# VectorE takes ten low-part subtractions of mixer 1 from GpSimd, woven between the conditioning sums

## The chip, the cores and the metric

The kernel runs on one core of one Trainium2 chip. The metric is the device time of one execution, in microseconds (us), median of several runs.

## What is computed

Two transformer blocks in a row, on 512 tokens of width 1024, all in float32. The part that this change touches is the end of the first block's mixer and the conditioning vector of the first block:

```python
mod = (c_act @ ada_w[l] + ada_b[l])[:, None, :]          # conditioning: 1024 -> 6144
sh_t, sc_t, g_t, sh_c, sc_c, g_c = jnp.split(mod, 6, axis=-1)
h = rms_norm(x, tm_pre_g[l]) * (1.0 + sc_t) + sh_t
...
gates = jax.nn.sigmoid(p["gate"] + merge_gate_b).reshape(Bn, S, N_BRANCH, D_MODEL)
merged = (gates[:, :, 0] * y_ml + gates[:, :, 1] * y_gla
          + gates[:, :, 2] * y_conf + gates[:, :, 3] * y_sc)
return merged @ w_o
```

## The kernel before, in words

**Units of weights.** Every large product runs over weight units of 128x2048 floats (1 MB). SP loads a unit into one of two buffers `w_raw` (512 KB per transfer, L481). ScalarE rounds it to the matmul format (`split`, L707, written `w_hi`), then VectorE or GpSimd computes the rest `w_lo = w_raw - w_hi`, its **low part** (`lo` in the kernel; L1731 on VectorE, L624 on GpSimd). TensorE multiplies high by high, high by low and low by high (L1209 to L1211: 48 matmuls of 512 columns per unit). Each buffer has two copies, so `w_hi` of unit u waits until TensorE has finished unit u-2 (`w_used`), and the load of unit u+2 waits for the low part of unit u (`parted`).

**The stage.** In program order the units here are `gate2` (4), `y2` (1), `gate0` (4), `y0` (1), `gate1` (4), `y1` (1), `wo` (4), then the feed-forward part `up1`. A `gate` unit yields two tiles of 128x512 in PSUM, which ScalarE opens with a sigmoid (`out_of`, L754). A `y` unit yields eight tiles; VectorE multiplies each with its gate (`gated`, L1982), which frees the PSUM bank, and adds it to `merged` (L1963). In `y1`, the last branch, ScalarE also rounds each merged tile (L953) and VectorE takes the merged tile's low part (L1968, `h_lo`), which `wo` needs. There are four PSUM banks for these tiles, so the fifth tile of a `y` unit waits for the product of the first.

**The conditioning sums.** The 6144 columns of `ada_w` are summed in 24 parts of 1 MB. Parts 0 to 7 are done at the start. Parts 8 to 23 are loaded by ScalarE's queue (L231, two transfers at a time, at places that the table `ADA_LOADED` gives), summed on VectorE (`ada_sum`: one L1769 and seven L1771 of 128x256 each, one after the other), and turned by TensorE (`ada_columns`, L1234, at places that `ADA_TURNED` gives). Four buffers hold parts, so loading part n from 12 on waits until TensorE has turned part n-4. TensorE waits in its own stream for a sum that isn't there.

**Who does what before.** GpSimd makes the low parts of all units from `y2` to the first `up1` unit. VectorE's queue has: `gated("y2")`, two `y_lo` subtractions, sums 8 to 13, `gated("y0")`, sums 14 to 21, `gated("y1")`, sums 22 and 23. All queues are in the order in which the code is written; nothing is reordered when it runs.

Of the kernel before, what the change touches and what calls it, by code (L numbers as in the profile page):

```python
# [149 lines left out]
def program(nc, A, out):  # L150
# [10 lines left out]
    with ctx:  # L161
        def sb(name, shape, dt=FP32):
            return ctx.enter_context(nc.sbuf_tensor(name, shape, dt))
# [3 lines left out]
        def sem(name):  # L167
            if name not in sems:
                sems[name] = ctx.enter_context(nc.semaphore(name))
            return sems[name]  # L170
# [9 lines left out]
        y_lo = sb("y_lo", [P, 4, S], F32R)  # L180
# [14 lines left out]
        def area(at, *shape):  # L195
            n = int(np.prod(shape))
            assert at + n <= WORK, (at, n)
            v = work[:, at:at + n]
            if len(shape) == 2:
                v = v.rearrange("p (a b) -> p a b", a=shape[0])  # L200
            if len(shape) == 3:
                v = v.rearrange("p (a b c) -> p a b c", a=shape[0], b=shape[1])
            return v
# [5 lines left out]
        def col(name, i=0, n=1):  # L209
            at = COLUMN[name]  # L210
            return par[:, at + i:at + i + n]
# [14 lines left out]
        def ada_place(n):  # L226

            return ada_first[n % 6] if n < 8 else ada_later[(n + 2) % 4]

        def ada_load(eng, n):  # L230
            eng.dma_start(ada_place(n), A["ada_w"][0][:, n * 2 * P:(n + 1) * 2 * P].rearrange("(k p) n -> p k n", p=P))\  # L231
               .then_inc(sem(f"ada_in{n % 8}"), 16)
# [7 lines left out]
        def vector_load(eng, g):  # L240
            r = 0
            for name, n in VECTORS[g]:
# [6 lines left out]
                else:  # L249
# [3 lines left out]

        ADA_LOADED = {(0, 0): (8, 9), (0, 1): (10, 11), (0, 2): (12, 13), (0, 4): (14, 15),
                      (1, 0): (16, 17), (1, 1): (18, 19), (1, 2): (20, 21), (1, 3): (22, 23)}
        ADA_TURNED = {(0, 2): (8, 9), (0, 3): (10, 11), (0, 4): (12, 13),
                      (1, 1): (14, 15), (1, 2): (16, 17), (1, 3): (18, 19), (1, 4): (20, 21)}
        ml_q, ml_k, ml_o = area(R, MT, S), area(R + 1024, MT, S), area(R + 2048, MT, S)  # L260
        ml_v = area(R + 3072, TT, MH * VW)
        ml_p, ml_h, ml_nm = area(R + 4128, 2, TT, S), area(R + 8224, TT, MIX), area(7232, S)
# [36 lines left out]
        def wait_full(eng, t, i=0):  # L299

            s, n, step = t.full
            eng.wait_ge(s, n + i * step)

        def wait_read(eng, t, i=0):

            eng.wait_ge(read[t.bank], t.n + i)
# [9 lines left out]
        def release(ins, t):  # L316
            ins.then_inc(read[t.bank], 1)
# [16 lines left out]
        U, unit = {}, 0  # L334
# [10 lines left out]
        def loaded_at(u):  # L345
            return 32 * (u // 2 + 1) + (16 if u >= IFA and (u - IFA) % 2 == 0 else 0)
# [260 lines left out]
        def _(pool):  # L607
# [13 lines left out]
            def lo(u):  # L621

                pool.wait_ge(hi_done, u + 1)
                pool.tensor_tensor(w_lo[u % 2][:, :], raw[u % 2][:, :], w_hi[u % 2][:, :].bitcast(FP32), ALU.subtract)\  # L624
                    .then_inc(parted[u % 2], 1)
# [20 lines left out]
                                       const("chunk_of").unsqueeze(2).broadcast_to([P, CPT, HD]), ALU.mult)\  # L646
                        .then_inc(sem("gl_placed"), 1)

            for u in range(U["y2"], U["up1"] + 1):
                lo(u)  # L650

            def hidden(n, conv_done):
# [45 lines left out]
        def _(act):  # L698
# [3 lines left out]
            def split(u, i=0, units=0):  # L702

                act.wait_ge(loaded[u % 2], loaded_at(u) + (i * 16 if units else 0))
                if u >= 2:
                    act.wait_ge(w_used, u - 1 + i)
                act.activation(w_hi[u % 2][:, :], raw[u % 2][:, :], ACT.Copy).then_inc(hi_done, 1)  # L707
# [41 lines left out]
            def out_of(t, dst, func, **kw):  # L749
                wait_full(act, t)  # L750
                src = bank[t.bank][:, :]
                if len(dst.shape) == 3:
                    src = src[:, 0:dst.shape[1] * dst.shape[2]].rearrange("p (a b) -> p a b", a=dst.shape[1])
                release(act.activation(dst, src, func, **kw), t)  # L754

            def gate_step(name, c, bias, u, used):

                split(u + 1)
                for k in range(2):
                    cc = 2 * c + k  # L760
                    if used is not None:
                        wait_read(act, T[used][cc])
                    out_of(T[name][cc], gates[:, cc, :], ACT.Sigmoid, **({} if bias is None else {"bias": col("merge_gate_b", bias + cc)}))
# [17 lines left out]
            u = U["sc"]  # L781
# [24 lines left out]
            u = U["ml"]  # L806
# [61 lines left out]
            u = U["gla"]  # L868
# [65 lines left out]
            def ada_more(b, c):  # L934

                for n in ADA_LOADED.get((b, c), ()):
                    if n == 8:
                        act.wait_ge(sem("y_lo"), 8)
                    if n >= 12:
                        act.wait_ge(sem("ada_turned"), n - 3)  # L940
                    ada_load(act, n)
# [260 lines left out]
        def _(pe):  # L1202
# [214 lines left out]
            def branch_unit(name, k0, n):  # L1417
                pe.wait_ge(sem("y_lo"), n)
                column_unit(U[name], T[name], 2, y_hi[:, k0:k0 + 2, :], y_lo[:, k0:k0 + 2, :])
# [90 lines left out]
            for k in range(2):  # L1510
                for c in range(4):
                    column_unit(U[f"gate{k}"] + c, T[f"gate{k}"][2 * c:2 * c + 2])
                    for p in ADA_TURNED.get((k, c), ()):
                        ada_columns(T["ada1"][0], p, 8)
                branch_unit(f"y{k}", 2 * k, 6 + 2 * k)
                for p in ADA_TURNED[(k, 4)]:
                    ada_columns(T["ada1"][0], p, 8)
# [207 lines left out]
        def _(dve):  # L1725
            ch = Chain(dve, "dve_step")

            def lo(u, i=0):

                dve.wait_ge(hi_done, u + 1 + i)  # L1730
                dve.tensor_tensor(w_lo[u % 2][:, :], raw[u % 2][:, :], w_hi[u % 2][:, :].bitcast(FP32), ALU.subtract)\  # L1731
                   .then_inc(parted[u % 2], 1)
# [33 lines left out]
            def ada_sum(n, unit):  # L1766

                dve.wait_ge(sem(f"ada_in{n % 8}"), 16 * (n // 8 + 1))
                ch.link(dve.tensor_scalar(unit[:, 0, :], unit[:, 0, :], c_act[:, 0:1], None, ALU.mult))  # L1769
                for k in range(1, KT):  # L1770
                    ins = dve.scalar_tensor_tensor(out=unit[:, 0, :], in0=unit[:, k, :], scalar=c_act[:, k:k + 1], in1=unit[:, 0, :],  # L1771
                                                   op0=ALU.mult, op1=ALU.add)
                    if k < KT - 1:
                        ch.link(ins)
                ins.then_inc(sem("ada_summed"), 1)
# [19 lines left out]
            u = U["sc"]  # L1795
# [160 lines left out]
            def product(c):  # L1956

                return rstd[:, :] if c % 3 == 2 else tbuf[:, c % 3, :]
# [8 lines left out]
                dve.wait_ge(sem("h_hi"), hn[0])  # L1967
                dve.tensor_tensor(h_lo[:, c, :], merged[:, c, :], h_hi[:, c, :].bitcast(FP32), ALU.subtract).then_inc(sem("h_ready"), 1)  # L1968

            def gated(name, bias=None, first=False, last=False):  # L1970

                for c in range(KT):
                    t = T[name][c]
                    wait_full(dve, t)
                    if GATE_OF[name] in ("gate2", "gp", "ga") or name == "y3" and c < KT - 1:
                        dve.wait_ge(sem(f"{GATE_OF[name]}_open"), c + 1)
                    else:
                        wait_read(dve, T[GATE_OF[name]][c])
                    dst = merged[:, c, :] if first else product(c)
                    if not first and gn[0] >= 2:  # L1980
                        dve.wait_ge(sem("added"), gn[0] - 1)
                    ins = dve.scalar_tensor_tensor(out=dst, in0=bank[t.bank][:, :], scalar=0.0 if bias is None else col(bias, c),  # L1982
                                                   in1=gates[:, c, :], op0=ALU.add, op1=ALU.mult)
                    release(ins, t)

                    if not first and c:
                        add(T[name][c - 1], c - 1)
                    if last and c >= 2:
                        merged_low(c - 2)
                if not first:  # L1990
                    add(T[name][KT - 1], KT - 1)
                if last:
                    for c in (KT - 2, KT - 1):
                        merged_low(c)
# [55 lines left out]
            for c in range(MT):  # L2050
# [17 lines left out]
                for hh in range(2):  # L2068
                    n = 2 * c + hh
# [6 lines left out]
                    release(dve.copy_predicated(gl_at[:, :, :], const("block_causal").bitcast(U32).unsqueeze(1).broadcast_to([P, TT, P]),  # L2076
                                                bank[t.bank][:, :].rearrange("p (a b) -> p a b", a=TT)), t)
            gla_norm(1)
            gated("y2", "conf_out_b")
            for k in range(2):  # L2080
                y_lo_of(gl_k[:, k, :], 2 + k, 7 + k)
            for n in range(8, 14):
                ada_sum(n, ada_place(n))
            gated("y0")
            for n in range(14, 22):
                ada_sum(n, ada_place(n))
            gated("y1", last=True)

            for n in (22, 23):
                ada_sum(n, ada_place(n))  # L2090
            ada_out(T["ada1"][0], 2 * KT, 4 * KT)
            wait_read(dve, T["ada1"][0])
            ch.tick(dve.tensor_tensor(gain[:, 1, :], mod[:, 2 * KT:3 * KT], col("tm_post_g", 0, KT), ALU.mult))
# [341 lines left out]
            for c in range(4):  # L2435
                for k in range(2):
                    t = T["wo2"][2 * c + k]
                    wait_full(dve, t)
                    n = 2 * c + k
# [59 lines left out]
```

## Time and profile before

| | us |
|---|---|
| median of 3 runs | 1729.02 |
| lowest, highest | 1725.0, 1729.88 |
| the profiled execution | 1726.85 |
| its span in the trace | 1724.9 |

The profiled execution is 2.2 us below the median. TensorE is busy for 95% of the span, VectorE for 55%, ScalarE for 35%, GpSimd for 18%. The mean granted TensorE clock is 0.967 of full speed. The stage of the change lies between about 398 and 560 us of the span. The views used are the list of waits, the timelines of the engines (start, length and, in square brackets, idle time before an instruction with what ended it), the chain of work that ended last, and the table by stretches.

### The profile page before, as it was taken

The page shows a single profiled execution, that of the slowest core. Times are in us where ns is not written, and L with a number is a line of the kernel's source. Part 1 is how long each engine was busy: PE and PEld are TensorE (multiplying, and loading weights), DVE is VectorE, ACT ScalarE, POOL GpSimd, SP SyncE. Part 2 cuts the span into 40 slices and gives each one's busy share as a digit, 9 for nine tenths or more (in the row PEclk, how much of TensorE's full clock was granted, in tenths as well). Part 3 has the DMA queues.
Part 4 walks back from the last instruction along what each step waited for, and adds up shares of the span by engine and source line. Part 5 has one row for each costly group of instructions (what it writes and reads, how often), then busy time and mean ns, then how long its engine had stood idle before and what let it go on. Part 6 is the DMA issues. An engine that isn't in the chain of part 4 may idle for free.

```text
span 1724.9 us, 19885 instructions
## 1 busy us (share of the span) xinstructions
PE 1636.9 (95%) x7592; PEld 1317.7 (76%) x7592; DVE 943.8 (55%) x1268; ACT 608.7 (35%) x758; POOL 310.0 (18%) x137
## 2 busy tenths in 40 slices
PE   5899999989899799999999899999999999999997
PEld 4688678768787578888888677877787888888886
DVE  4449456424989554444433657866434655556333
ACT  2342444224223443333322422344443433334222
POOL 0330013323343201111000000244353111111000
PEclk8799999988999999999999999999999999999999
DMA  8323122303764213333222224322122333332221
GB/s 284 108 79 99 49 74 74 94 30 108 234 225 134 79 51 97 97 97 97 98 98 97 74 77 124 90 74 74 50 74 75 108 98 97 97 97 97 98 97 49
DMA packets 192139, 170.41 MB, mean 99 GB/s; under 512 B 9413, under 2 KB 180973, under 8 KB 192077
## 3 DMA queue, kind: packets, MB, share of 16 engines
q1 hardware_dynamic: 174669, 150.39, 28.5%
q10 hardware_dynamic: 16800, 16.83, 3.1%
q0 software_dynamic: 608, 2.35, 0.4%
q8 instruction: 42, 0.69, 0.2%
q14 instruction: 20, 0.16, 0.0%
HBM read 165.54 MB, written 2.10 MB: 97 GB/s over the span
## 4 chain that ended last, share of the span: by engine, by line
PE 82%; DVE 10%; ACT 2%; issue 2%; SPq 2%; DMA 1%; POOL 0%; DVEq 0%; ACTq 0%
PE bank L1209 24%; PE bank L1211 23%; PE bank L1210 23%; DVE work L1771 4%; PE bank L1234 1%; SPq L231 1%; PE bank L1216 1%; DVE work L1834 1%; PE bank L1218 1%; PE bank L1217 1%; PE bank L1670 1%; ACT w_hi L707 1%; PE bank L1478 1%; PE bank L1308 1%; DVE w_lo L1731 1%
## 5 line engine op out<-in xcount | busy, mean ns | idle before, releaser
L1209 PE MATMUL bank<-h_hi,w_hi 128*128 128x512 f32 x1536 | 614.7, 400 | 26.3 <-DVE h_lo L1749 12.4
L1211 PE MATMUL bank<-h_hi,w_lo 128*128 128x512 f32 x1536 | 603.7, 393 | 0.0
L1210 PE MATMUL bank<-h_lo,w_hi 128*128 128x512 f32 x1536 | 603.7, 393 | 0.0
L1209 PEld LDWEIGHTS bank<-h_hi,w_hi 128*128 128x128 f32 x1536 | 291.9, 190 | 112.4 <-issue 38.6
L707 ACT ACTIVATE w_hi<-w_raw 128x2048 fp32r<-128x2048 f32 x131 | 250.1, 1909 | 304.8 <-PE bank L1211 257.3
L1211 PEld LDWEIGHTS bank<-h_hi,w_lo 128*128 128x128 f32 x1536 | 291.7, 190 | 62.7
L1210 PEld LDWEIGHTS bank<-h_lo,w_hi 128*128 128x128 f32 x1536 | 292.1, 190 | 59.3 <-issue 1.0
L1731 DVE TENSOR_TENSOR w_lo<-w_raw,w_hi 128x2048 fp32r<-128x2048 f32 x86 | 198.0, 2302 | 244.5 <-ACT w_hi L707 244.2
L624 POOL TENSOR_TENSOR w_lo<-w_raw,w_hi 128x2048 fp32r<-128x2048 f32 x45 | 210.0, 4666 | 513.1 <-ACT w_hi L707 512.9
L1209 PE MATMUL bank<-y_hi,w_hi 128*128 128x512 f32 x480 | 192.4, 401 | 13.1 <-DVE tbuf L1982 8.2
L1211 PE MATMUL bank<-y_hi,w_lo 128*128 128x512 f32 x480 | 189.7, 395 | 0.0
L1210 PE MATMUL bank<-y_lo,w_hi 128*128 128x512 f32 x480 | 189.7, 395 | 0.0
L660 POOL TENSOR_TENSOR work<-work 128x512 f32 x44 | 57.1, 1298 | 458.1 <-ACT work L1018 458.1
L1209 PEld LDWEIGHTS bank<-y_hi,w_hi 128*128 128x128 f32 x480 | 92.1, 192 | 36.1 <-DVE tbuf L1982 9.1
L1771 DVE SCALAR_TENSOR_TENSOR work<-work,small 128x256 f32<-128x256 f32 x154 | 112.8, 733 | 5.5
L1210 PEld LDWEIGHTS bank<-y_lo,w_hi 128*128 128x128 f32 x480 | 92.1, 192 | 19.5 <-issue 0.5
L1211 PEld LDWEIGHTS bank<-y_hi,w_lo 128*128 128x128 f32 x480 | 91.9, 191 | 19.6
L2166 DVE SCALAR_TENSOR_TENSOR work<-bank,par,work 128x511 f32<-128x511 f32 (+1 forms) x88 | 61.5, 743 | 77.8 <-ACT work L1012 77.8
L1012 ACT ACTIVATE work<-work,par 128x512 f32<-128x512 f32 x44 | 35.8, 815 | 106.8 <-DVE work L2155 106.8
L1012 ACT ACTIVATE work<-bank,par 128x512 f32<-128x512 f32 x44 | 30.0, 687 | 107.3 <-PE bank L1211 107.1
L2166 DVE SCALAR_TENSOR_TENSOR work<-work,par 128x511 f32<-128x511 f32 (+1 forms) x88 | 61.9, 746 | 9.6 <-ACT work L1012 9.6
L754 ACT ACTIVATE work<-bank,par 128x512 f32<-128x512 f32 x32 | 22.0, 687 | 119.1 <-PE bank L1211 119.1
(249 smaller groups left out, 1384.5 us busy)
## 6 DMA issues: line engine op xcount, KB each, us to landing
w_raw<-in_w_in SPq DMA_DIRECT2D x94, 512.0 KB, 4.7
w_raw<-in_ffn_w_up SPq DMA_DIRECT2D x44, 512.0 KB, 4.7
w_raw<-in_w_up SPq DMA_DIRECT2D x44, 512.0 KB, 4.9
work<-in_ada_w ACTq DMA_DIRECT2D x16, 1024.0 KB, 7.3
w_raw<-in_ffn_w_down SPq DMA_DIRECT2D x22, 512.0 KB, 3.9
w_raw<-in_w_down SPq DMA_DIRECT2D x22, 512.0 KB, 4.0
work<-in_ada_w SPq DMA_DIRECT2D x8, 1024.0 KB, 12.0
w_raw<-in_w_o SPq DMA_DIRECT2D x8, 512.0 KB, 4.0
```

The source lines that it names most:

```text
L231: eng.dma_start(ada_place(n), A["ada_w"][0][:, n * 2 * P:(n + 1) * 2 * P].rearrange("(k p) n -> p k n", p=P))\
L624: pool.tensor_tensor(w_lo[u % 2][:, :], raw[u % 2][:, :], w_hi[u % 2][:, :].bitcast(FP32), ALU.subtract)\
L660: pool.tensor_tensor(work[:, bass.ds(i * (2 * S) + k * S, S)], cbuf[:, k, 0, :], cbuf[:, k, 1, :], ALU.mult).then_inc(sem("hid" + n), 1)
L707: act.activation(w_hi[u % 2][:, :], raw[u % 2][:, :], ACT.Copy).then_inc(hi_done, 1)
L754: release(act.activation(dst, src, func, **kw), t)
L1012: act.activation(cbuf[:, k, part, :], src, ACT.Identity, scale=par[:, bass.ds(i * 2 + at, 1)], **kw).then_inc(sem("center" + n), 1)
L1209: pe.matmul(dst, w_hi[s][:, at:at + n], hi, start=first, stop=False)
L1210: pe.matmul(dst, w_hi[s][:, at:at + n], lo, start=False, stop=False)
L1211: return pe.matmul(dst, w_lo[s][:, at:at + n], hi, start=False, stop=last)
L1731: dve.tensor_tensor(w_lo[u % 2][:, :], raw[u % 2][:, :], w_hi[u % 2][:, :].bitcast(FP32), ALU.subtract)\
L1771: ins = dve.scalar_tensor_tensor(out=unit[:, 0, :], in0=unit[:, k, :], scalar=c_act[:, k:k + 1], in1=unit[:, 0, :], op0=ALU.mult, op1=ALU.add)
L2166: ins = dve.scalar_tensor_tensor(out=c[:, back:S], in0=src[:, 0:S - back], scalar=w, in1=c[:, back:S], op0=ALU.mult, op1=ALU.add)
```

## The change

VectorE now makes the low parts of eleven units in a row: `gate0` (4), `y0`, `gate1` (4), `y1` and the first of `wo`. GpSimd keeps `y2`, the other three of `wo` and the first of `up1`. On VectorE each low part stands between pairs of sums, and the low parts of `gate0`'s, `gate1`'s and `wo`'s first units stand inside `gated`, behind the fourth tile's product. The sums are the same 16, in other places: six between `y2` and `y0`, eight between `y0` and `y1`, two behind `y1`. The transfers of parts 8 and 9 are issued by ScalarE ahead of the first `gate0` tile, as soon as the two `y_lo` are there; those of 10 to 23 follow at earlier places than before or the same. TensorE turns parts 8 and 9 one unit earlier, and parts 14 to 21 as one, two, two, two, one in place of four pairs.

```diff
-        ADA_LOADED = {(0, 0): (8, 9), (0, 1): (10, 11), (0, 2): (12, 13), (0, 4): (14, 15),
-                      (1, 0): (16, 17), (1, 1): (18, 19), (1, 2): (20, 21), (1, 3): (22, 23)}
-        ADA_TURNED = {(0, 2): (8, 9), (0, 3): (10, 11), (0, 4): (12, 13),
-                      (1, 1): (14, 15), (1, 2): (16, 17), (1, 3): (18, 19), (1, 4): (20, 21)}
+        ADA_LOADED = {(0, 0): (10, 11), (0, 1): (12, 13), (0, 2): (14, 15), (0, 3): (16, 17),
+                      (1, 0): (18,), (1, 1): (19, 20), (1, 2): (21, 22), (1, 3): (23,)}
+        ADA_TURNED = {(0, 1): (8, 9), (0, 2): (10, 11), (0, 3): (12, 13), (0, 4): (),
+                      (1, 0): (14,), (1, 1): (15, 16), (1, 2): (17, 18), (1, 3): (19, 20), (1, 4): (21,)}
...
-            for u in range(U["y2"], U["up1"] + 1):
+            lo(U["y2"])
+            for u in range(U["wo"] + 1, U["up1"] + 1):
                 lo(u)
...
                 split(u + 1)
+                if u == U["gate0"]:
+                    act.wait_ge(sem("y_lo"), 8)
+                    for n in (8, 9):
+                        ada_load(act, n)
...
                     release(ins, t)
+                    if low_at and c == 3:
+                        lo(low_at)
...
-            gated("y2", "conf_out_b")
+            gated("y2", "conf_out_b", low_at=U["gate0"])
...
-            for n in range(8, 14):
-                ada_sum(n, ada_place(n))
-            gated("y0")
-            for n in range(14, 22):
-                ada_sum(n, ada_place(n))
-            gated("y1", last=True)
+            lo(U["gate0"] + 1)
+            sums(8, 9)
+            lo(U["gate0"] + 2)
+            sums(10, 11)
+            lo(U["gate0"] + 3)
+            sums(12, 13)
+            lo(U["y0"])
+            gated("y0", low_at=U["gate1"])
+            lo(U["gate1"] + 1)
+            sums(14, 15)
+            lo(U["gate1"] + 2)
+            sums(16, 17)
+            lo(U["gate1"] + 3)
+            sums(18, 19)
+            lo(U["y1"])
+            sums(20, 21)
+            gated("y1", last=True, low_at=U["wo"])
```

On VectorE, between the `y_lo` subtractions and the first product of `y0`, there stood six sums in a row (each a TENSOR_SCALAR and seven SCALAR_TENSOR_TENSOR); here the end of them, with the first product of `y0`:

```order
L1756 TENSOR_TENSOR y_lo<-work,y_hi 128x512 x2
L1769 TENSOR_SCALAR work<-work,small 128x256
L1771 SCALAR_TENSOR_TENSOR work<-work,small 128x256 x7
L1769 TENSOR_SCALAR work<-work,small 128x256
L1771 SCALAR_TENSOR_TENSOR work<-work,small 128x256 x7
...
L1982 SCALAR_TENSOR_TENSOR tbuf<-bank3,work 128x512
```

In the changed kernel the same place on VectorE reads (L1734 is the low part, L1772 and L1774 the sum, L1985 the product):

```order
L1759 TENSOR_TENSOR y_lo<-work,y_hi 128x512 x2
L1734 TENSOR_TENSOR w_lo1<-w_raw1,w_hi1 128x2048
L1772 TENSOR_SCALAR work<-work,small 128x256
L1774 SCALAR_TENSOR_TENSOR work<-work,small 128x256 x7
L1772 TENSOR_SCALAR work<-work,small 128x256
L1774 SCALAR_TENSOR_TENSOR work<-work,small 128x256 x7
L1734 TENSOR_TENSOR w_lo0<-w_raw0,w_hi0 128x2048
...
L1734 TENSOR_TENSOR w_lo0<-w_raw0,w_hi0 128x2048
L1985 SCALAR_TENSOR_TENSOR tbuf<-bank3,work 128x512
```

Four low parts (`gate0` units 1 to 3 and `y0`) now stand in that stretch, one ahead of each pair of sums and one behind the last.

On VectorE in the last branch, `gated("y1")`, a product, an addition (L1966) and a merged tile's low part (L1971) alternate; behind the fourth product stands now the low part of the first `wo` unit:

```order
L1985 SCALAR_TENSOR_TENSOR tbuf<-bank2,work 128x512
L1734 TENSOR_TENSOR w_lo0<-w_raw0,w_hi0 128x2048
L1966 TENSOR_TENSOR work<-work,rstd 128x512
L1971 TENSOR_TENSOR h_lo<-work,h_hi 128x512
L1985 SCALAR_TENSOR_TENSOR tbuf<-bank3,work 128x512
```

Before, the addition followed the product at once.

## Rows read from the trace of the kernel before

**Rows 1.** Waits of TensorE, 400 to 600 us: total, times, longest (us)
```profile
PE bank L1209 <- DVE tbuf L1982: 8.2, 2, 4.6
```
**Rows 2.** TensorE's timeline, unit `y0`: start, length, line, idle before
```profile
454.75 0.48 PE L1209 MATMUL bank<-y_hi,w_hi 128*128 128x512 f32 x1
...
465.03 0.50 PE L1209 MATMUL bank<-y_hi,w_hi 128*128 128x512 f32 x1 [4.55 <-DVE tbuf L1982]
...
465.96 0.63 PE L1209 MATMUL bank<-y_hi,w_hi 128*128 128x512 f32 x1
466.39 0.63 PE L1210 MATMUL bank<-y_lo,w_hi 128*128 128x512 f32 x1
...
472.20 0.95 PE L1234 MATMUL bank<-small,work 128*128 128x1 f32 x8
```
**Rows 3.** TensorE's timeline, unit `y1`
```profile
519.37 0.48 PE L1209 MATMUL bank<-y_hi,w_hi 128*128 128x512 f32 x1
...
528.76 0.79 PE L1209 MATMUL bank<-y_hi,w_hi 128*128 128x512 f32 x1 [3.66 <-DVE tbuf L1982]
...
536.76 0.95 PE L1234 MATMUL bank<-small,work 128*128 128x1 f32 x8
```
**Rows 4.** VectorE's timeline: first sum, one sum, first products, last addition
```profile
427.47 1.04 DVE L1769 TENSOR_SCALAR work<-work,small 128x256 f32<-128x256 f32 x1 [12.92 <-DMA work<-in_ada_w]
...
440.60 3.61 DVE L1771 SCALAR_TENSOR_TENSOR work<-work,small 128x256 f32<-128x256 f32 x7
...
464.29 1.28 DVE L1982 SCALAR_TENSOR_TENSOR tbuf<-bank,work 128x512 f32<-128x512 f32 x2
...
520.34 7.76 DVE L1771 SCALAR_TENSOR_TENSOR work<-work,small 128x256 f32<-128x256 f32 x7
...
540.64 0.68 DVE L1963 TENSOR_TENSOR work<-work,tbuf 128x512 f32<-128x512 f32 x1
```
**Rows 5.** GpSimd's timeline: three of its eleven low parts in this stage
```profile
445.76 4.75 POOL L624 TENSOR_TENSOR w_lo<-w_raw,w_hi 128x2048 fp32r<-128x2048 f32 x1 [6.25 <-ACT w_hi L707]
...
523.16 4.66 POOL L624 TENSOR_TENSOR w_lo<-w_raw,w_hi 128x2048 fp32r<-128x2048 f32 x1 [7.83 <-ACT w_hi L707]
543.87 4.61 POOL L624 TENSOR_TENSOR w_lo<-w_raw,w_hi 128x2048 fp32r<-128x2048 f32 x1 [16.05 <-ACT w_hi L707]
```
**Rows 6.** The chain of work that ended last: start, length, what
```profile
446.07 4.73 DVE work L1771
```
**Rows 7.** ScalarE's timeline: transfers issued, sigmoid, weights rounded
```profile
420.63 1.04 ACTq L231 DMA_DIRECT2D work<-in_ada_w  x2
...
431.50 1.01 ACTq L231 DMA_DIRECT2D work<-in_ada_w  x2
...
507.00 0.69 ACT L754 ACTIVATE work<-bank,par 128x512 f32<-128x512 f32 x1 [4.76 <-PE bank L1211]
...
508.68 1.92 ACT L707 ACTIVATE w_hi<-w_raw 128x2048 fp32r<-128x2048 f32 x1 [0.99 <-PE bank L1234]
...
541.89 1.90 ACT L707 ACTIVATE w_hi<-w_raw 128x2048 fp32r<-128x2048 f32 x1
```
**Rows 8.** The page's costliest groups: the low part on VectorE, mean ns
```profile
L1731 DVE TENSOR_TENSOR w_lo<-w_raw,w_hi 128x2048 fp32r<-128x2048 f32 x86 | 198.0, 2302 | 244.5 <-ACT w_hi L707 244.2
```
**Rows 9.** Transfers of `ada_w`, issue to landing
```profile
DMA to landing us min/median/max: 5.1/8.1/13.9
```
**Rows 10.** Waits of TensorE elsewhere, and the clock behind one (stretch: length, busy, ..., PEclk, DMA share, GB/s)
```profile
148.83 0.39 PE L1216 MATMUL bank<-w_hi,h_hi 128*128 128x256 f32 x1 [1.72 <-DVE w_lo L1731]
...
1050.30 0.70 PE L1614 MATMUL bank<-work 64*128 64x256 f32 x4 [2.30 <-issue]
...
1313.29 0.80 PE L1209 MATMUL bank<-h_hi,w_hi 128*128 128x512 f32 x1 [3.39 <-POOL w_lo L624]
...
1314.00:1319.00 5.00, 5.00 (x14) 3.86 (x12) 0.00 (x0) 0.00 (x0) 3.88 (x1) 0.50 0.62 210
```
**Rows 11.** Table by stretches (same columns: PE, PEld, DVE, ACT, POOL busy)
```profile
435.00:445.00 10.00, 10.00 (x50) 8.40 (x49) 9.64 (x13) 2.62 (x3) 4.50 (x1) 1.00 0.89 273
```

More of the change, by code:

```diff
@@ L936, in ada_more @@
                 for n in ADA_LOADED.get((b, c), ()):
-                    if n == 8:
-                        act.wait_ge(sem("y_lo"), 8)
                     if n >= 12:
@@ L1968, in merged_low, with gated @@
                 dve.tensor_tensor(h_lo[:, c, :], merged[:, c, :], h_hi[:, c, :].bitcast(FP32), ALU.subtract).then_inc(sem("h_ready"), 1)
-            def gated(name, bias=None, first=False, last=False):
+            def gated(name, bias=None, first=False, last=False, low_at=None):
                 for c in range(KT):
@@ L2078, in _, with sums @@
             gla_norm(1)
-            gated("y2", "conf_out_b")
+            gated("y2", "conf_out_b", low_at=U["gate0"])
             for k in range(2):
                 y_lo_of(gl_k[:, k, :], 2 + k, 7 + k)
-            for n in range(8, 14):
-                ada_sum(n, ada_place(n))
-            gated("y0")
-            for n in range(14, 22):
-                ada_sum(n, ada_place(n))
-            gated("y1", last=True)
-            for n in (22, 23):
-                ada_sum(n, ada_place(n))
+            def sums(*parts):
+                for n in parts:
+                    ada_sum(n, ada_place(n))
+            lo(U["gate0"] + 1)
[15 more added lines that the diff above has]
+            gated("y1", last=True, low_at=U["wo"])
+            sums(22, 23)
             ada_out(T["ada1"][0], 2 * KT, 4 * KT)
```

## The prediction, made before the changed kernel ran

> **What bounds the kernel now.** I read the busy shares first: TensorE is the bound of the whole kernel, so a change gains only where TensorE stands still or runs slowly. The list of TensorE's waits [rows 1] shows that in this stage it waits twice for VectorE, 8.2 us in all, both times for a product of a branch tile. TensorE's timeline puts the first wait into unit y0 (4.55 us idle, [rows 2]) and the second into y1 (3.66 us idle, [rows 3]): four tiles fill the four banks, and the fifth needs a bank that VectorE hasn't freed. Behind each wait the matmuls start 0.43 us apart for a while (465.96 to 466.39, [rows 2]), where an undisturbed unit of 48 in 10.9 us has them 0.23 apart: the clock is at 1.2 GHz there and not at 2.4, as the granted clock of 0.50 behind another wait shows [rows 10]. So each unit costs more than its idle time: y0 runs from 454.75 to the turned parts at 472.20, 17.45 us; y1 from 519.37 to 536.76, 17.4 us. Undisturbed, a unit of 48 matmuls takes 10.9 us (two issues by ScalarE, each at the end of a gate unit, are 431.50 - 420.63 = 10.87 apart, [rows 7]). **Each branch unit loses 6.5 us, 13.0 together.**
>
> Why is VectorE late? Its first product of y0 starts at 464.29, straight behind the sums; the same in y1 behind the sum at 520.34 [rows 4]. An undisturbed sum is 0.3 + 3.61 = 3.9 us (row at 440.60). But about every second one takes 7.8: the chain shows a single step of 4.73 us at 446.07 [rows 6] where its neighbours take 0.50. GpSimd's low part began at 445.76 and ended at 450.51 [rows 5], the step ended at 450.80. The last such step lies at 523 to 528: the sum begun at 520.34 ends only at 528.1, GpSimd's low part at 523.16 ends at 527.82. So **VectorE stands still for about 4.2 us of each of GpSimd's 4.6 us low parts**, whenever they meet. A second cause is the late start: the first sum begins at 427.47 after 12.92 us of idle time, since its transfer is issued at 420.63 [rows 4, 7].
>
> The Trainium skill's page "SBUF — State Buffer" (section Terms) says the same of the pair of ports that VectorE and GpSimd share: one holds it for a whole instruction and the other is blocked, not slowed. By this rule the trace agrees, with 4.73 against 0.50.
>
> **The change part by part.**
>
> *Low parts on VectorE.* One costs 2.3 us there [rows 8] and 4.6 on GpSimd, plus 4.2 of stall. Per gate unit VectorE now has two sums and a low part, 2 x 3.9 + 2.3 = 10.1 us, against 10.9 for TensorE (11.8 with two parts turned, at 0.95). It keeps up, with 0.8 to 1.7 us to spare per unit. Before, two sums took 3.9 + 7.8 = 11.7 us.
>
> *The earlier transfers.* They are issued when the two y_lo are there. VectorE has those at 414.55 (427.47 less the idle 12.92), and the low part of gate0's first unit inside gated(y2) replaces a stall of the same size, so I take 414.8. Landing took 5.1 (minimum) to 8.1 us (median) [rows 9], so the first sum starts at 419.9 to 422.9; I take 421.5, since the one ahead of it took 6.8 with more traffic beside it.
>
> *First tight place.* The low part of gate0's third unit is queued behind sums 8 and 9, and TensorE is queued behind that: 421.5 + 7.8 + 2.3 = 431.6. TensorE ends the second unit at 431.2 and turns parts 8 and 9 to 432.15. It fits with 0.5; at 422.9 TensorE waits 0.9. I take nothing.
>
> *Next units.* Sums 10, 11 end at 439.4, the next low part at 441.7 (needed near 444), sums 12, 13 at 449.5, y0's low part at 451.8 (needed at 455.7). VectorE is idle when y0 starts at 454.75 + 0.95 (one pair is turned ahead of it instead of behind) = 455.7. Each product follows its tile. **Gone: 6.5 us.** y0 ends at 466.6.
>
> *gate1.* Before, four units with three pairs took 519.37 - 473.0 = 46.4; now there is half a pair more: y1 starts at 466.6 + 46.4 + 0.45 = 513.45. VectorE's last low part before it, y1's, waits for ScalarE: the rounding starts 1.7 us behind the second sigmoid of gate1's third unit and takes 1.9 (508.68 behind 507.00, [rows 7]); that unit ends at 500.8, so VectorE starts at 504.7, ends the low part at 507.0 and sums 20, 21 at 514.8. The first tile of y1 is there at 515. **The second stall is gone too: 6.5 us.** TensorE would begin wo 13 us earlier, near 524.9.
>
> *What is late next.* In gated(y1) VectorE does three operations per tile at 0.60 us start to start (two products of 0.68 take 1.28, row at 464.29, [rows 4]): 1.8 us, against 1.36 per tile on TensorE. Before, all that was hidden behind the stall. From the third product (its tile is ready at 517.75) to the last addition there are 18 operations, 10.8 us, and now the low part of wo's first unit, 2.2: the last addition starts at 530.75, against 540.64. **That is 9.9 us earlier, not 13.** ScalarE rounds wo's second unit only behind the last merged tile (541.89 before), and GpSimd takes its low part from then (543.87 to 548.48, [rows 5, 7]). Before, TensorE was ready for that unit at the same moment. Now TensorE is done with wo's first unit at 524.9 + 10.9 + 0.4 (it waits that long for the bank of y1's sixth tile) = 536.2, and the low part is there 9.9 us earlier than 548.5, at 538.6. So a new wait of 2.4 us stands in front of wo's second unit. Whether it costs the clock too: waits of 1.72 and 2.30 us left the next matmuls fast, one of 3.39 was followed by a clock of 0.50 for 5 us, and those of 3.66 and 4.55 by slow matmuls too [rows 10, 2, 3]. 2.4 is nearest to 2.30, so I take no loss; the other bound is 12 slow matmuls at 0.20, 2.5 us.
>
> The Trainium skill ("TensorE: Matmul & The Clock Gate", HAM oscillation) warns that waits between groups of matmuls can put the clock back. [...]
>
> *The rest.* Sums 22 and 23 still meet GpSimd's low parts but end before 552, and TensorE turns them behind wo's third unit near 560. Everything behind is moved as a whole. **Sum: 13.0 - 0.4 - 2.4 and some tenths for the moved parts, 9.9 us, set by the chain over VectorE, ScalarE and GpSimd.**
>
> **The rivals.**
>
> *A: the clock falls at the new wait*, as above, or TensorE waits some tenths at the tight place as well. Gain 7.0 to 7.4, time 1720.7. For it: at 3.39 it fell. Chance 0.2.
>
> *B: a transfer lands late.* Low parts are queued behind sums, and a sum behind its transfer. The longest landing was 13.9 us [rows 9]. At the first sum that would be 414.8 + 13.9 + 10.1 = 438.8, 6.7 behind what TensorE needs, and the clock's 2.5 on top: gain near 1, time 1727. For part 21 (issued at 501.9, landed 515.8) it would cost 3.5. Against it: the median is 8.1, and the part of the first sum took 6.8 before, beside a weight unit. Chance 0.1, half of it within 0.3%.
>
> *C: the stretched steps don't come from GpSimd* but from the transfers that run beside them. Then two sums still take 11.7 us, and with a low part 14.0 against 11.8 per unit: VectorE is the bound and TensorE waits 2.2 us at every unit, since it now needs low parts from the same queue. y0 starts at 421.5 + 3 x 14.0 = 463.5 and ends at 474.4, VectorE is through its products some 3 us later, 477.5, and four periods of 14.0 bring it to 533.5 for the products of y1, which before began at 528.1: 5.4 us later. 1726.85 + 5.4 = 1732.3, with half of the 2.2 between profile and median 1733, **slower**. It decides from about 4.8 us per sum on (11.8 - 2.3, halved). Against it: the sum at 440.60 ran at full speed while the transfers took 0.89 of the DMA engines [rows 11]. The skill's SBUF page says too that engines and transfers don't share ports. Chance 0.03.
>
> *D: it doesn't do what it says*: ScalarE, which waits for turned parts before its transfers and rounds behind them, TensorE and VectorE hold each other up in a ring, so that the branch units still start their products late. The slack that I find in the ring is 0.5 us at the first place and about 1.3 at y1. If it were eaten at each of the eight units by 1 us, 8 of the 9.9 us were lost: 1726, within 0.3%. Chance 0.05.
>
> **How the numbers follow.** The profiled execution took 1726.85 us; less 9.9 it is 1717.0. It lies 2.2 below the median of its runs, 1729.02; less 9.9 that is 1719.1. I take the middle, 1718.0, as the forecast, chance 0.62. For the range: the fastest run, 1725.0, less 12.6 (the new wait absent) is 1712.4; the median less 5.5 is 1723.5, which takes in A with both its terms and part of B. A measurement of this kernel can tell about 0.3%, 5.2 us. Faster by more: 0.62 + 0.2 + 0.05 = 0.87. Within: B's other half and D, 0.1. Slower: 0.03.
>
> **What would show each step right or wrong.** TensorE's waits for L1985 in y0 and y1 are gone, and y0 and y1 take about 11 us each. No step of a sum takes over 1 us until GpSimd's low part of wo's second unit. VectorE's first sum starts near 421. A new wait for GpSimd's low part, about 2.4 us, stands in front of wo's second unit; if it is absent, the gain is over 10. A wait in front of gate0's third unit would be the tight place. If steps of 4.7 us stay in the sums while GpSimd is idle, the whole is wrong and C holds.

## The result and the profile after

The changed kernel takes 1717.48 us (median of 6 runs, 1714.17 to 1719.16), the kernel before 1727.12 us (median of 6, 1725.0 to 1729.88). The ratio is 0.994 with a 95% interval of 0.9927 to 0.9954: 9.6 us faster. The profiled execution took 1717.51 us, with a span of 1715.7; before it was 1726.85 and 1724.9. The forecast was 1718.0, and the time lies in its range.

The page shows what moved. The low part on VectorE is now there 97 times instead of 86 ([rows 8]), at the same price, and GpSimd is left with 34 of 45: eleven low parts have moved, and not ten as the title has it.

```profile
PE 1633.3 (95%) x7592; PEld 1314.8 (77%) x7592; DVE 933.6 (54%) x1279; ACT 608.6 (35%) x758; POOL 257.0 (15%) x126
...
L1734 DVE TENSOR_TENSOR w_lo<-w_raw,w_hi 128x2048 fp32r<-128x2048 f32 x97 | 223.1, 2300 | 248.4 <-ACT w_hi L708 248.1
...
L624 POOL TENSOR_TENSOR w_lo<-w_raw,w_hi 128x2048 fp32r<-128x2048 f32 x34 | 157.0, 4617 | 556.4 <-ACT w_hi L708 556.3
```

TensorE's waits between 400 and 600 us (total, times, longest) answer to [rows 1]. The 8.2 us for VectorE's products are down to 0.4, and a wait for GpSimd is new:

```profile
PE bank L1212 <- POOL w_lo L624: 2.0, 1, 2.0
...
PE bank L1212 <- DVE rstd L1985: 0.4, 1, 0.4
```

TensorE's timeline (start, length, line, operation, idle before it) shows both branch units, and `wo`'s first two. It answers to [rows 2, 3]:

```profile
454.49 0.48 PE L1212 MATMUL bank<-y_hi,w_hi 128*128 128x512 f32 x1
...
465.49 0.39 PE L1212 MATMUL bank<-h_hi,w_hi 128*128 128x512 f32 x1
...
512.23 0.48 PE L1212 MATMUL bank<-y_hi,w_hi 128*128 128x512 f32 x1
...
523.24 0.50 PE L1237 MATMUL bank<-small,work 128*128 128x1 f32 x4
...
524.99 0.50 PE L1212 MATMUL bank<-h_hi,w_hi 128*128 128x512 f32 x1 [0.44 <-DVE rstd L1985]
...
537.52 0.50 PE L1212 MATMUL bank<-h_hi,w_hi 128*128 128x512 f32 x1 [2.04 <-POOL w_lo L624]
537.86 0.53 PE L1213 MATMUL bank<-h_lo,w_hi 128*128 128x512 f32 x1
538.18 0.63 PE L1214 MATMUL bank<-h_hi,w_lo 128*128 128x512 f32 x1
538.61 0.63 PE L1212 MATMUL bank<-h_hi,w_hi 128*128 128x512 f32 x1
```

`y0` runs from 454.49 to the first matmul of `gate1` at 465.49, and `y1` from 512.23 to the turned half pair at 523.24: 11.0 us each, where it was 17.4. Behind the new wait the matmuls of 0.63 us lie 0.43 us apart, up to 540.74: TensorE has fallen to 1.2 GHz, which the table by stretches confirms (length, busy of PE, PEld, DVE, ACT, POOL, then the granted clock, DMA share, GB/s):

```profile
538.00:540.00 2.00, 2.00 (x7) 1.53 (x6) 1.93 (x3) 0.70 (x1) 1.22 (x1) 0.50 0.70 192
540.00:542.00 2.00, 2.00 (x8) 1.59 (x7) 2.00 (x1) 0.00 (x0) 2.00 (x1) 0.66 1.00 341
```

VectorE's timeline, beside [rows 4]. The seven long steps of every one of the fourteen sums up to `y1` take their undisturbed 3.61 us, and the first one begins at 419.00 instead of 427.47:

```profile
419.00 0.35 DVE L1772 TENSOR_SCALAR work<-work,small 128x256 f32<-128x256 f32 x1 [3.39 <-DMA work<-in_ada_w]
...
427.15 2.28 DVE L1734 TENSOR_TENSOR w_lo<-w_raw,w_hi 128x2048 fp32r<-128x2048 f32 x1
...
456.15 0.69 DVE L1985 SCALAR_TENSOR_TENSOR tbuf<-bank,work 128x512 f32<-128x512 f32 x1 [6.67 <-PE bank L1214]
...
513.89 0.69 DVE L1985 SCALAR_TENSOR_TENSOR tbuf<-bank,work 128x512 f32<-128x512 f32 x1 [0.52 <-PE bank L1214]
...
529.65 0.69 DVE L1966 TENSOR_TENSOR work<-work,tbuf 128x512 f32<-128x512 f32 x1
...
532.04 12.12 DVE L1774 SCALAR_TENSOR_TENSOR work<-work,small 128x256 f32<-128x256 f32 x7
```

When `y0`'s first tile is there, VectorE has been idle for 6.67 us, where before it was still at its sums. The last row is the sum of part 22, which still meets low parts on GpSimd, two of them (532.89 and 538.78, 4.57 and 4.58 us), and takes 12.12 us instead of 3.61. Nobody waits for it.

### The profile page after: what moved, and what is told of

It reads as the page before. It is cut to its first block, busy times and chain, and to the rows that moved or that the text cites. A ratio compares the mean times of both kernels' runs of the same rounds, so it can differ in the third digit from the quotient of the medians.

```text
span 1715.7 us, 19885 instructions
## 1 busy us (share of the span) xinstructions
PE 1633.3 (95%) x7592; PEld 1314.8 (77%) x7592; DVE 933.6 (54%) x1279; ACT 608.6 (35%) x758; POOL 257.0 (15%) x126
## 4 chain that ended last, share of the span: by engine, by line
PE 85%; DVE 7%; ACT 2%; SPq 2%; issue 2%; POOL 1%; DMA 1%; DVEq 0%; ACTq 0%
PE bank L1212 25%; PE bank L1214 25%; PE bank L1213 24%; PE bank L1237 1%; SPq L231 1%; ACT w_hi L708 1%; PE bank L1219 1%; DVE work L1837 1%; DVE w_lo L1734 1%; PE bank L1220 1%; PE bank L1221 1%; PE bank L1673 1%; PE bank L1481 1%; PE bank L1311 1%; PE bank L1658 1%
## 5 line engine op out<-in xcount | busy, mean ns | idle before, releaser
L1734 DVE TENSOR_TENSOR w_lo<-w_raw,w_hi 128x2048 fp32r<-128x2048 f32 x97 | 223.1, 2300 | 248.4 <-ACT w_hi L708 248.1
L624 POOL TENSOR_TENSOR w_lo<-w_raw,w_hi 128x2048 fp32r<-128x2048 f32 x34 | 157.0, 4617 | 556.4 <-ACT w_hi L708 556.3
L1774 DVE SCALAR_TENSOR_TENSOR work<-work,small 128x256 f32<-128x256 f32 x154 | 83.2, 540 | 5.5
```

## The experiments

The kernels ran in three groups, each beside runs of the kernel before: the first is the result above (before 1727.12 us); the second is the two halves, the kernel with GpSimd beside and the changed kernel again (1728.32, 24 runs); the third is the last four rows of the table (1725.4, 11 runs). A time is to be read against its own group. Because the executions differ by a few us at places that no kernel here touches, I also give a length in the trace of the one profiled execution: from the matmul in front of which TensorE waits 1.18 us for ScalarE (`y2`, 394.69 before) to the one behind a wait of 0.73 us (583.16 before). I call it the stage. "Slow" are matmuls of about 0.6 us in place of 0.39, counted in the stage; each puts 0.43 us between two starts instead of 0.23, so it costs 0.20.

| kernel | median us | ratio to before, 95% | stage us | slow in `y2` | slow behind it |
|---|---|---|---|---|---|
| before | 1727.12 / 1728.32 / 1725.4 | | 188.47 | 9 | 18 |
| changed | 1717.48 | 0.9927 to 0.9954 | 178.91 | 2 | 7 |
| changed, again | 1716.56 | 0.992 to 0.9957 | 178.85 | 2 | 8 |
| low parts alone | 1729.29 | 0.9996 to 1.0019 | 191.80 | 2 | 28 |
| transfers alone | 1721.23 | 0.9951 to 0.9975 | 184.50 | 2 | 5 |
| GpSimd beside | 1723.10 | 0.9962 to 0.9981 | 184.93 | 1 | 8 |
| changed, third | 1717.69 | 0.9934 to 0.996 | 179.00 | 2 | 8 |
| `wo`'s second low part on VectorE | 1711.67 | 0.9897 to 0.9927 | 176.26 | 8 | 0 |
| and `wo`'s first one earlier | 1711.51 | 0.99 to 0.9926 | 175.58 | 8 | 0 |
| `wo`'s first one earlier, alone | 1714.16 | 0.9912 to 0.994 | 178.06 | 2 | 8 |

### Is it the low parts or the transfers?

The kernel before with the low parts on VectorE as in the change, and the transfers left where they were:

```diff
 (tables of the transfers and ScalarE's wait as before)
-            for u in range(U["y2"], U["up1"] + 1):
+            lo(U["y2"])
+            for u in range(U["wo"] + 1, U["up1"] + 1):
...
+            lo(U["gate0"] + 1)
+            sums(8, 9)
+            lo(U["gate0"] + 2)
+            sums(10, 11)
```

> The changed kernel with the transfers of the conditioning parts and the places where TensorE turns them as in the kernel before; VectorE still makes the eleven low parts. My theory (VectorE is in order, and the earlier transfers are what makes the first low part fit): the first sum starts near 426.5 us, the low part of gate0's third unit ends at 426.5 + 7.8 + 2.3 = 436.6, TensorE needs it at 430 and waits about 6 us in front of that unit, with 2.5 us at the low clock behind it. No wait in y0 and y1. About 8 to 9 us slower than the changed kernel, so 1725.5 to 1726.5 us, level with the kernel before. Rival (all of the gain comes from taking the low parts off GpSimd, the transfers matter little): within 3 us of the changed kernel, 1718 to 1720 us.

It measured 1729.29 us: no gain at all, and 12.7 us more than the changed kernel beside it (1716.56), where 8 to 9 were expected. TensorE's, VectorE's and ScalarE's timelines say why:

```profile
436.98 0.80 PE L1210 MATMUL bank<-h_hi,w_hi 128*128 128x512 f32 x1 [4.80 <-DVE w_lo L1732]
466.11 0.76 PE L1210 MATMUL bank<-y_hi,w_hi 128*128 128x512 f32 x1 [3.40 <-issue]
```
```profile
426.81 0.35 DVE L1770 TENSOR_SCALAR work<-work,small 128x256 f32<-128x256 f32 x1 [9.19 <-DMA work<-in_ada_w]
...
434.64 2.28 DVE L1732 TENSOR_TENSOR w_lo<-w_raw,w_hi 128x2048 fp32r<-128x2048 f32 x1
...
455.90 0.35 DVE L1770 TENSOR_SCALAR work<-work,small 128x256 f32<-128x256 f32 x1 [8.29 <-DMA work<-in_ada_w]
456.29 3.61 DVE L1772 SCALAR_TENSOR_TENSOR work<-work,small 128x256 f32<-128x256 f32 x7
...
463.73 2.28 DVE L1732 TENSOR_TENSOR w_lo<-w_raw,w_hi 128x2048 fp32r<-128x2048 f32 x1
```
```profile
450.47 1.01 ACTq L231 DMA_DIRECT2D work<-in_ada_w  x2
```

The stretched sums and the waits for products are gone, but the low part of `gate0`'s third unit stands in VectorE's queue behind two sums, and those behind a transfer that lands at 426.8. It ends at 436.9, and TensorE waits 4.80 us for it. The same again in front of `y0`: sums 12 and 13 wait 8.29 us for their transfer, and `y0`'s low part ends at 466.01; TensorE starts 0.10 us behind it, so I put the 3.40 us down to it, although the timeline names no releaser. The second wait follows from the first: the transfer of parts 12 and 13 goes out only when TensorE has turned 8 and 9, at 450.47 here and at 442.65 in the kernel before. I had expected one such wait and a time level with the kernel before; there were two, each with slow matmuls behind it. **On VectorE a low part inherits the lateness of every transfer ahead of it.**

The other half, the transfers alone (the low parts stay on GpSimd):

```diff
-        ADA_LOADED = {(0, 0): (8, 9), (0, 1): (10, 11), ...
+        ADA_LOADED = {(0, 0): (10, 11), (0, 1): (12, 13), ...
 (ADA_TURNED as in the change)
...
+                if u == U["gate0"]:
+                    act.wait_ge(sem("y_lo"), 8)
+                    for n in (8, 9):
+                        ada_load(act, n)
```

> The kernel before with only the new places of transfers and of turned parts; GpSimd keeps all low parts. My theory: the first sum starts near 419 instead of 427.5, so VectorE gets to y0's products at about 456 and the wait in y0 is gone (6.5 us), but 53.8 us of sums stretched by GpSimd stand between y0's products and y1's, so the wait in y1 grows by 1 to 3 us: the products of y1 start near 523, 5 us earlier than before. Total 1722 us, 5 us faster than before. Steps of 4.7 us stay in the sums. Rival (the earlier transfers alone bring the whole gain): 1718 us, no wait in y1. Other rival (they bring nothing): 1727 us.

It measured 1721.23 us, within a microsecond of what was expected; against its own group that is a gain of 7.1 us where 5 were expected. VectorE's timeline shows the stretched sums, every second one, and GpSimd's what they meet:

```profile
420.85 7.84 DVE L1773 SCALAR_TENSOR_TENSOR work<-work,small 128x256 f32<-128x256 f32 x7
...
428.98 3.61 DVE L1773 SCALAR_TENSOR_TENSOR work<-work,small 128x256 f32<-128x256 f32 x7
...
432.89 7.83 DVE L1773 SCALAR_TENSOR_TENSOR work<-work,small 128x256 f32<-128x256 f32 x7
...
460.86 4.14 DVE L1965 TENSOR_TENSOR work<-work,tbuf 128x512 f32<-128x512 f32 x1
```
```profile
412.61 7.03 POOL L624 TENSOR_TENSOR w_lo<-w_raw,w_hi 128x2048 fp32r<-128x2048 f32 x1 [7.36 <-ACT w_hi L707]
423.69 4.71 POOL L624 TENSOR_TENSOR w_lo<-w_raw,w_hi 128x2048 fp32r<-128x2048 f32 x1 [4.05 <-ACT w_hi L707]
435.76 4.68 POOL L624 TENSOR_TENSOR w_lo<-w_raw,w_hi 128x2048 fp32r<-128x2048 f32 x1 [7.36 <-ACT w_hi L707]
```

TensorE's timeline has what is left of the waits for products:

```profile
525.43 0.80 PE L1211 MATMUL bank<-y_hi,w_hi 128*128 128x512 f32 x1 [2.51 <-DVE tbuf L1984]
```

The early start alone gets the sums done before `y0` and removes that wait. In `y1` one of 2.51 us is left, where I had expected the 3.66 to grow by 1 to 3, and TensorE waits twice for a sum that it is to turn (1.01 and 1.02). So the two halves aren't a sum of gains: transfers alone 7.1 us (1728.32 - 1721.23), low parts alone none, both 11.8 in this group (1728.32 - 1716.56). The earlier transfers pay by themselves, and they are what makes the low parts on VectorE pay.

### Is it GpSimd that stretches the sums?

The changed kernel, and beside it GpSimd, once per unit from `gate0`'s second to `y1` (nine times), subtracts 128x1536 constants from themselves into room that nobody reads:

```diff
+            wait_read(pool, T["gl_ms"][1])
+            pool.wait_ge(sem("y_src"), 6)
+            for u in range(U["gate0"] + 1, U["y1"] + 1):
+                pool.wait_ge(hi_done, u + 1)
+                pool.tensor_tensor(work[:, 16384:16384 + 1536], cst[:, 0:1536], cst[:, 0:1536], ALU.subtract).then_inc(sem("beside"), 1)
+                pool.wait_ge(sem("beside"), u - U["gate0"])
```

> The changed kernel, with nine subtractions of 128x1536 added on GpSimd, at the moments at which it would have begun its low parts (gate0's second unit to y1); they read constants and write a free area, nobody reads the result or waits for it. Theory (GpSimd holds something that VectorE needs for its whole instruction): a step of the sums is 3 us longer at each meeting, VectorE needs 13.2 us per unit where TensorE needs 11.8, TensorE waits in front of gate0's third unit and in y1, and the kernel takes 1727 to 1731 us. Rival (the long steps came from the transfers, or from both engines reading the same weight buffers): no long step, and 1716 to 1719 us like the changed kernel.

It measured 1723.10 us, 6.5 slower than the changed kernel in the same group, and 4 faster than the low end of what I expected: a meeting cost VectorE 2.1 to 2.6 us where I had taken 3, and the chain had more slack than I had reckoned with. Its profiled execution (1718.2) is the fastest of its ten, though its stage is 6.1 us longer than the changed kernel's; the rest of that execution was quicker, and the stage and the median agree. The sums that meet one are stretched again, by VectorE's timeline and GpSimd's:

```profile
422.67 2.47 DVE L1778 TENSOR_SCALAR work<-work,small 128x256 f32<-128x256 f32 x1 [0.29 <-DMA work<-in_ada_w]
425.18 3.61 DVE L1780 SCALAR_TENSOR_TENSOR work<-work,small 128x256 f32<-128x256 f32 x7
...
431.29 5.97 DVE L1780 SCALAR_TENSOR_TENSOR work<-work,small 128x256 f32<-128x256 f32 x7
...
443.68 6.17 DVE L1780 SCALAR_TENSOR_TENSOR work<-work,small 128x256 f32<-128x256 f32 x7
```
```profile
433.66 2.81 POOL L654 TENSOR_TENSOR work<-cst 128x1536 f32<-128x1536 f32 x1 [8.67 <-ACT w_hi L714]
445.78 2.75 POOL L654 TENSOR_TENSOR work<-cst 128x1536 f32<-128x1536 f32 x1 [9.32 <-ACT w_hi L714]
```

5.97 less 3.61 is 2.36 of the 2.81 us, and 6.17 less 3.61 is 2.56 of the 2.75. The first row is a sum's opening instruction, else 0.35 us, beside the operation that GpSimd began at 422.21. The transfers are those of the changed kernel, whose sums all take 3.61, and GpSimd reads constants here and no weights. That settles rival C: the stretch comes from GpSimd, not from the transfers and not from a weight buffer that both engines read. It also shows how little room the chain has: 2.4 us more per unit bring back waits for sums to turn (2.7 us in four), for low parts (0.9 in two) and for the bank of a tile of `y1` (0.8).

### What does the new wait cost?

The changed kernel again, for its spread:

> The changed kernel once more, unchanged, to see which parts of its trace repeat. Theory: a time of 1715 to 1719.5 us; the wait for GpSimd's low part in front of wo's second unit is there again with about 2 us, and the matmuls behind it are slow (0.43 us apart) in some executions and not in others. Rival: the slow matmuls behind it are there each time, 8 or more.

It measured 1716.56 us. The wait in front of `wo`'s second unit is 2.04 us again, with 8 slow matmuls behind it. Then three variants of the end of the stage and the changed kernel beside them.

`wo`'s second low part on VectorE, behind the last merged low part:

```diff
-            for u in range(U["wo"] + 1, U["up1"] + 1):
+            for u in range(U["wo"] + 2, U["up1"] + 1):
...
             gated("y1", last=True, low_at=U["wo"])
+            lo(U["wo"] + 1)
             sums(22, 23)
```

> The changed kernel with one low part more on VectorE: that of wo's second unit, right behind gated(y1); GpSimd begins with wo's third unit. Theory: the 2.04 us wait for GpSimd in front of wo's second unit and the slow matmuls behind it are one cost of 2.0 + 8 x 0.20 = 3.6 us, and nothing behind it takes their place. The rounding ends near 532.8 on the scale of the changed kernel's trace, VectorE takes 2.3 us to 535.1, TensorE is done with wo's first unit at 535.5: no wait, no matmul over 0.40 us at the start of wo's second unit, whole kernel 3.6 us faster than the changed kernel, near 1713.3. Rival 1: the slow matmuls come from something else (the bank wait of 0.44, or load) and stay: 2.0 us faster, near 1714.9. Rival 2: a later wait takes it back (sums 22 and 23 end 3.4 us later on VectorE, TensorE turns them behind wo's third unit): same time as the changed kernel, with a wait for a sum near 560.

It measured 1711.67 us, 6.0 less than the changed kernel beside it (1717.69); the two intervals allow some 3 us either way, so that the expected 3.6 is among them. The wait is gone, and no slow matmul is left behind `y2`. VectorE's timeline shows the low part, which ends at 534.97; by TensorE's the last matmul of `wo`'s first unit starts at 534.93 and the next unit follows at the usual distance:

```profile
532.68 2.29 DVE L1734 TENSOR_TENSOR w_lo<-w_raw,w_hi 128x2048 fp32r<-128x2048 f32 x1 [1.11 <-ACT w_hi L708]
534.89 0.35 DVE L1772 TENSOR_SCALAR work<-work,small 128x256 f32<-128x256 f32 x1
```
```profile
534.93 0.39 PE L1214 MATMUL bank<-h_hi,w_lo 128*128 128x512 f32 x1
535.16 0.40 PE L1212 MATMUL bank<-h_hi,w_hi 128*128 128x512 f32 x1
```

The stage is the finer measure: 176.26 against 178.91, 2.65 shorter, although this execution had 8 slow matmuls in `y2` where the other had 2. At 0.20 each that is 1.2, and the edit itself is worth 3.85: the wait with 2.2 (the two matmuls around it start 2.43 apart instead of 0.23) and the slow matmuls with 1.6. Rival 1 (they stay) and rival 2 (a later wait takes it back) are both out.

The same kernel with the order in `gated(y1)` changed too, the low part of `wo`'s first unit behind the first product instead of the fourth:

```diff
-                    if low_at and c == 3:
+                    if low_at and c == (0 if last else 3):
```

> As the kernel with wo's second low part on VectorE, and in gated(y1) the low part of wo's first unit behind the first product instead of the fourth, where VectorE was idle 0.69 us. Theory: the chain of 18 operations and a low part becomes one of 18 operations alone from the third product on, the last addition comes 0.9 us earlier (about 528.7 for 529.65), and the 0.44 us wait for the bank of y1's fifth or sixth tile is gone: 4.0 us faster than the changed kernel, near 1712.9. Rival: the second product is now 1.5 us late (516.8 for 515.3), TensorE waits for its bank by 0.3 us or more, and the result is that of the kernel without this edit.

1711.51 us: the median can't be told from the one without it (1711.67). The stage is 0.68 us shorter and the wait of 0.44 is gone, so the edit does what it should, at a size that only the trace resolves. Its median is the lowest of the kernels here, 0.8% below the kernel before.

The same line alone, with GpSimd keeping `wo`'s second unit:

> The changed kernel with only the order in gated(y1) changed: low part of wo's first unit behind the first product; GpSimd keeps wo's second unit. TensorE reaches wo's second unit 0.44 us earlier, GpSimd's low part is ready 0.95 us earlier: the wait shrinks from 2.04 to about 1.5 us. It is meant to place the clock's loss: waits of 2.04, 2.04, 2.04 and 2.08 were each followed by about 8 slow matmuls, one of 1.23 by none. Theory: the wait itself decides, and at 1.5 the matmuls stay at 0.23 us spacing: gain 0.95 + 1.6 = 2.5, near 1714.4. Rival: it isn't the length (the load behind the wait falls the clock anyway): slow matmuls again, gain 0.95, near 1716.

It measured 1714.16 us. That is the number of the theory (1714.4), but the trace decides for the rival: the stage is only 0.85 us shorter than the changed kernel's (178.91), the slow matmuls are there, and most of the 3.5 us between the medians (1717.69 - 1714.16) lies outside the stage. The wait shrank to 1.80 only and not to 1.5: the low part came 0.85 us earlier, but TensorE came 0.6 earlier too, since the 0.44 us wait that fell away had cost 0.6 start to start. TensorE's timeline behind it:

```profile
537.42 0.50 PE L1212 MATMUL bank<-h_hi,w_hi 128*128 128x512 f32 x1 [1.80 <-POOL w_lo L624]
537.75 0.39 PE L1213 MATMUL bank<-h_lo,w_hi 128*128 128x512 f32 x1
...
538.91 0.62 PE L1212 MATMUL bank<-h_hi,w_hi 128*128 128x512 f32 x1
539.33 0.63 PE L1213 MATMUL bank<-h_lo,w_hi 128*128 128x512 f32 x1
```

Slow matmuls again, 8 of them, after six fast ones. So in front of this unit waits of 2.04 (three times), 2.04 and 2.08 (low parts alone, GpSimd beside) and 1.80 us all led to 7 or 8 slow matmuls, and one of 1.23 us (transfers alone) to none. That places no threshold: the 1.18 us in `y2` had up to 9 slow matmuls behind it, and 1.72 and 2.30 elsewhere had none ([rows 10]). The length of the wait alone doesn't decide, and the runs don't say what does.

The changed kernel beside them:

> The changed kernel itself, on the same chip as the three others, for comparison: near 1716.9, with a wait of about 2.0 us for GpSimd in front of wo's second unit and about 8 matmuls 0.43 us apart behind it.

1717.69 us, a wait of 2.04 and 8 slow matmuls, as expected.

## Why the prediction was right, and where it wasn't

*What bounds, and the two stalls: right.* Both branch units take 11.0 us (10.9 forecast), and both waits for products are gone. The cause was named rightly too: no sum up to `y1` is stretched once GpSimd is idle, and the sums that meet it again, with GpSimd's operation put back, are.

*The positions: right, up to a constant.* `y0` started at 454.49 (455.7 forecast, behind one pair more, since all of parts 8 to 13 are turned one unit earlier and not only 8 and 9), `y1` at 512.23 (513.45), the last addition at 529.65 (530.75), and GpSimd's low part was ready at 537.46 (538.6). Each is 1.1 to 1.2 earlier than the forecast. That constant isn't the change's. It comes from `y2`, where the two executions part at about 398, ahead of every moved instruction (the first is a low part, on GpSimd at 400.03 before and on VectorE at 403.68 after): behind the wait of 1.18 us the execution before had 9 slow matmuls and the one after 2, 7 x 0.20 = 1.4 us. The table by stretches, first of before and then of after:

```profile
398.50:401.00 2.50, 2.50 (x7) 1.93 (x7) 1.79 (x3) 1.46 (x1) 0.97 (x1) 0.54 0.02 7
```
```profile
398.50:401.00 2.50, 2.50 (x12) 2.04 (x11) 2.47 (x4) 1.62 (x1) 0.00 (x0) 1.00 0.03 7
```

The change isn't its cause as far as the runs show: two variants had 8 there with the same instructions up to that point as the changed kernel, which had 2 in three executions, and the kernel with the transfers alone had 2 with all of GpSimd's low parts in place. It was not settled what decides it.

*The tight place: slack underrated.* The transfers were issued at 413.44 and the first sum began 5.6 us later; I had taken 6.7. The low part of `gate0`'s third unit ended at 429.43, and TensorE's next unit began 1.4 us behind it, where 0.5 was forecast. The run with GpSimd beside it (the second sum 2.1 us longer, TensorE waits 0.49 there) shows the place to be as described. In `gate1` VectorE waited for ScalarE's rounding, 1.79 us in front of `y1`'s low part, as the forecast had it.

*The new wait: right, and mis-sized in one term.* It was forecast at 2.4 and is 2.04: that is idle time, and from start to start it costs 2.2. **The step that failed is "I take no loss" of the clock.** I had placed 2.4 by the row nearest to it, 2.30, which showed fast matmuls; at this place the clock fell in all three executions of the changed kernel, for 1.6 us. This is the mechanism of rival A, at two thirds of its price (2.5). The row at 2.30 is a matmul of another kind, 64x256, and at another place; nearness in length alone was no reason to choose it over the one at 3.39. The Trainium skill ("TensorE: Matmul & The Clock Gate", A second HAM failure mode: psum-queue depth-cycling) describes a kernel in which frequent short idle times between groups of matmuls made the clock swing between its two levels. The traces here go further: a single wait of 1.80 or 2.04 us was followed by slow matmuls.

*Why the time came out right all the same.* With the loss the sum would be 13.0 - 0.6 - 2.2 - 1.6 = 8.6. The stages of the traces, 188.47 and 178.91, differ by 9.56, of which 1.4 is `y2`: 8.2 for the change. The medians of the three groups differ by 9.6, 11.8 and 7.7. So a trace of each says 8.2, the medians 7.7 to 11.8, and my 9.9 lies inside that without being confirmed to the microsecond: the 1.6 that I left out is of the size of what executions differ by. That the measured 1717.48 lies half a microsecond from the forecast is luck: in the profiled pair the 1.4 us of `y2` stands in for most of the 1.6.

*The rivals.* B (late transfer) did not occur. Its longest landing was a misreading: 13.9 us and the median of 8.1 are over all 24 transfers; the eight at the start of the kernel took 5.3 to 13.9, and the sixteen of this stage 5.1 to 9.3, median 7.3, in the trace of before, and up to 11.2 in that of the changed kernel. C is refuted by the run with GpSimd's operation. D, the ring, did not show in the changed kernel, where no low part and no sum kept TensorE waiting up to `y1`. With the transfers late (low parts alone) both B's chain and D's ring are there: the 4.80 us wait for a low part delays the turning, that the next transfer, and that brings the second wait, and the change brought nothing.

## What to carry to other kernels

When work moves to a queue that also waits for transfers, place the transfers first: the moved instructions inherit every late landing ahead of them, and here the half without the transfers gained nothing. Count GpSimd's elementwise operations twice, once for GpSimd and once for VectorE, where they meet VectorE operations like the sums here: a low part of 4.6 us on GpSimd cost VectorE 4.2. And after a stall is removed, follow the chain to the next wait and move that too: one low part more, behind the products, was worth 3.85 us in the trace, nearly half of the 8.2 that the eleven and the earlier transfers had brought.

## What the runs showed of the hardware

- Which of the two engines stands still isn't fixed. With the transfers alone, GpSimd's low part at 412.61 took 7.03 us instead of 4.6 while VectorE's additions and subtractions ran at full speed up to 415.16 (the last two are in the row below); the one at 423.69 took 4.71, and the sum beside it 4.2 more. The Trainium skill ("SBUF — State Buffer", SBUF: two separate sides) says that whichever starts first holds the shared pair of ports for its whole instruction. Both rows fit: at 412.61 VectorE was already at work, and 412.61 + 7.03 - 4.6 = 415.0 is where its run of four ended. By this reckoning GpSimd waited out the whole run, and not one instruction of it. The runs don't say why at 423.69 it got in between two steps of a sum, and here not between two of the four.

```profile
413.88 1.28 DVE L1758 TENSOR_TENSOR y_lo<-work,y_hi 128x512 fp32r<-128x512 f32 x2
```

- One and the same wait can have very different clock losses. Behind the 1.18 us wait in `y2` there were 1, 2, 8 or 9 slow matmuls in ten executions, and behind one of 3.97 us some 200 us later 10 in the traces of before and of the changed kernel, and 5 to 8 in the variants (a first matmul of up to 0.77 us is not counted). That alone moves a run by a microsecond or more, so edits of that size are better read from a stretch of the trace than from the total.
- A short wait costs more than its idle time: 0.44 us of idle put 0.84 us between two matmuls that are else 0.23 apart, a loss of 0.6; 2.04 put 2.43, a loss of 2.2.
